# Attention stage scheduled in units of one pair of score maps, and its large loads issued by ScalarE

## What is computed

```
# sb (stick-breaking): 4 heads of 64
z = q k^T / 8
log_keep = where(k < q, log_sigmoid(-z), 0)
a = where(k < q, exp(log_sigmoid(z) + sum of log_keep over later keys), 0);   o = a v
# df (differential): 4 heads with two maps of 32 columns each
s = q_c k_c^T / sqrt(32) + bias;  p_c = softmax(s, chunk mask);   o = rmsnorm((p_0 - lam p_1) v) * g
# ds (top-k sparse): s = q k^T / 8 + bias, softmax over the keys the indexer chose
# fx (forgetting): s = q k^T / 8 + decay, causal softmax
x = x + concat(o_sb, o_df, o_ds, o_fx) w_out
```

## Time and profile before

| | us |
|---|---|
| median of 3 runs | 3913.75 (3907.92 to 3913.81) |
| the profiled execution's own time | 3915.1 |
| its span | 3913.3 |
| PE busy in the span | 3586.7 (92%) |
| DVE busy | 2494.6 (64%) |
| ACT busy | 1063.1 (27%) |
| attention, first layer | 662 to 1097 |
| attention, second layer | 2564 to 2998 |

### The profile page before, as it was taken

The page is one execution under the profiler, slowest core; times in us unless marked ns, Lnnn a source line. Parts: engine busy times, 40 slices in busy tenths (PEclk is TensorE's granted clock), DMA queues, the critical chain, the costliest instruction groups (busy, mean ns, idle before and its releaser), DMA issues. The chain is left out here.

```text
span 3913.3 us, 53493 instructions
## 1 busy us (share of the span) xinstructions
PE 3586.7 (92%) x19553; PEld 2727.3 (70%) x19553; DVE 2494.6 (64%) x4584; ACT 1063.1 (27%) x2223; POOL 34.4 (1%) x160
## 2 busy tenths in 40 slices
PE   4999998989878999999969999989998799999995
PEld 2554554656558999999935555555565699999994
DVE  3288996575654666655636899936655566655655
ACT  3111122565532111111111112145544311111112
POOL 0000000000000000000000000000000000000000
PEclk7999999899999999999989999988999899999997
DMA  4111214101001111111011221131100111111101
GB/s 164 69 41 64 69 41 160 62 7 48 20 11 60 49 48 36 45 48 48 12 63 55 69 70 43 59 121 59 48 12 23 44 46 35 48 48 48 48 27 45
DMA packets 216658, 206.69 MB, mean 53 GB/s; under 512 B 23846, under 2 KB 193158, under 8 KB 214430
## 3 DMA queue, kind: packets, MB, share of 16 engines
q1 hardware_dynamic: 216478, 204.36, 16.1%
HBM read 159.41 MB, written 44.91 MB: 52 GB/s over the span
## 5 line engine op out<-in xcount | busy, mean ns | idle before, releaser
L1614 PE MATMUL psum<-h_split,gate_up_split 128*128 128x352 f32 x6336 | 1021.5, 322 | 44.2 <-DVE gate_up_split L1728 44.2
L1614 PEld LDWEIGHTS psum<-h_split,gate_up_split 128*128 128x128 f32 x6336 | 1013.5, 189 | 48.3 <-issue 46.9
L882 PE MATMUL psum<-arena 128*128 128x512 f32 (+4 forms) x2304 | 756.1, 486 | 0.0
L1758 DVE TENSOR_TENSOR arena<-arena,psum 128x352 f32<-128x352 f32 x1056 | 513.6, 521 | 318.0 <-PE psum L1614 318.0
L882 PEld LDWEIGHTS psum<-arena 128*128 128x128 f32 (+1 forms) x2304 | 413.0, 181 | 329.2 <-issue 290.8
L1614 PE MATMUL psum<-hid_split,down_split 128*128 128x352 f32 x3168 | 522.9, 325 | 11.1 <-DVE down_split L1728 11.1
L1614 PEld LDWEIGHTS psum<-hid_split,down_split 128*128 128x128 f32 x3168 | 516.4, 190 | 11.6 <-issue 11.6
L1021 DVE MAX8 top<-arena 128x8 f32<-128x384 f32 (+6 forms) x394 | 346.7, 880 | 13.5
L1022 DVE MATCH_REPLACE8 arena<-top,arena 128x384 f32<-128x384 f32 (+6 forms) x394 | 339.0, 861 | 0.0
L1484 DVE CUSTOM_DVE_ANT_0 arena<-psum,arena 128x128 f32<-128x128 f32 (+8 forms) x288 | 194.7, 705 | 194.4 <-PE psum L1250 88.2
L1250 PE MATMUL psum<-arena 64*128 64x512 f32 (+9 forms) x1040 | 226.7, 543 | 65.2 <-ACT arena L1395 34.0
(11 more groups left out here) (139 smaller groups left out, 2748.2 us busy)
## 6 DMA issues: line engine op xcount, KB each, us to landing
gate_up_raw<-in_w_gate SPq DMA_DIRECT2D x44, 512.0 KB, 3.7
gate_up_raw<-in_w_up SPq DMA_DIRECT2D x44, 512.0 KB, 4.7
down_raw<-in_w_down SPq DMA_DIRECT2D x44, 512.0 KB, 3.5
arena<-in_w_in SPq DMA_DIRECT2D x24, 768.0 KB, 6.7
arena<-k_turned SPq DMA_DIRECT2D x8, 1184.0 KB, 5.7
k_turned<-arena SPq DMA_DIRECT2D x72, 128.0 KB, 2.2
q_turned<-arena SPq DMA_DIRECT2D x64, 128.0 KB, 2.1
arena<-bias_strips SPq DMA_DIRECT2D x4, 2048.0 KB, 10.2
```

The costliest lines, as they stand in the source:

```text
L882: ins = nc.tensor.matmul(m.ps[0:n, o + n0:o + n1], m.hT[:, c, c0:c0 + n], w[:, c, n0:n1], start=(c == 0), stop=(c == KC - 1))
L1614: ins = nc.tensor.matmul(out, w[i], x[k], start=(first and n == 0), stop=(last and n == 2))
L1758: nc.vector.tensor_tensor(x, x, bank(m, down_bank[p])[:, 0:PIECE], ALU.add).then_inc(s.added, 1)
```

## The change

A unit of one pair of maps (in df: one head) becomes the step of every loop. There are 90: ds 0 to 17, df 18 to 53, fx 54 to 71, sb 72 to 89. Scores run two units ahead (`AHEAD`), the weights (exp, combine, scan and multiply) one; sb's sigmoids, which free the score banks, also run two ahead. For that `soft` becomes a ring of four, the scan works in place in it and `back` goes. The fillers are spread over units 21 to 52 and 60 to 81. The group loads and `w_out` are issued by ACT: df and two parts before its loop, fx at unit 24, a part and sb at unit 57, the last part at unit 84. SP keeps the q blocks. The sigmoid set is asked for at v = 70, the iteration in which unit 72's sigmoids begin.

```diff
-FILLED = dict(ds=(21, 36), df=(41, 62))
+FILLED = dict(ds=(21, 53), df=(60, 82))
+AHEAD = 2
...
+                    for part in range(2 if g == "df" else 1):
+                        heads = [part] if g == "df" else [0, 1]
+                        self.units.append(Unit(len(self.units), st, heads, x, part == 1 or g != "df"))
+                        x += 2
...
@@ sync @@
             for e in range(3):
                 load_q(e)
-            load_group("df", 1, l)(sp, s.group_in1)
-            for g in ("ds", "df"):
-                load_w_out(m, a, l, g)(sp, w_out_in[W_OUT_SLOT[g]])
-            for e in range(3, n_steps // 2):
-                if e == 14:
...
-                    load_group("fx", 0, l)(sp, s.group_in0)
-                if e == 23:
...
-                    load_group("sb", 1, l)(sp, s.group_in1)
-                if e == 24:
...
-                    load_w_out(m, a, l, "fx")(sp, s.w_out_in0)
+            for e in range(3, len(steps) // 2):
+                sp.wait_ge(s.scored, 2 * steps[2 * (e - 2)].unit0)
                 load_q(e)
...
@@ tensor @@
-            for j in range(-1, n_steps + FLUSH):
-                scores(plan.step(j + 1), 0)
-                turn_probs(plan.step(j), 0)
-                weighted_sum(plan.step(j - 1), 0)
-                scores(plan.step(j + 1), 1)
-                turn_probs(plan.step(j), 1)
-                weighted_sum(plan.step(j - 1), 1)
-                sum_squares(plan.ended_at(j - 3, "df"))
-                turn_recips(plan.ended_at(j - 1, "ds", "df", "fx"))
-                products(j)
+            for v in range(-AHEAD, plan.n_units + FLUSH):
+                scores(plan.unit(v + AHEAD))
+                turn_probs(plan.unit(v), 0)
+                weighted_sum(plan.unit(v - 1), 0)
+                turn_probs(plan.unit(v), 1)
+                weighted_sum(plan.unit(v - 1), 1)
+                sum_squares(plan.ended_at(v - 3, "df"))
+                turn_recips(plan.ended_at(v - 1, "ds", "df", "fx"))
+                products(v)
...
@@ scalar @@
-            def weights(st, part):
...
+            def weights(v, c):
+                u = plan.unit(v + 1)
+                if u and u.st.g != "sb":
+                    exp(u, c)
+                u = plan.unit(v + AHEAD)
+                if u and u.st.g == "sb":
+                    sticks(u, c)
...
+            load_group("df", 1, l)(nc.scalar, s.group_in1)
+            for g in ("ds", "df"):
+                load_w_out(m, a, l, g)(nc.scalar, w_out_in[W_OUT_SLOT[g]])
+            for v in range(-AHEAD, plan.n_units + FLUSH):
+                if v + AHEAD < plan.n_units and units[v + AHEAD].v == plan.first_stick // 2:
                     act.preload_act_table_set("sigmoid_and_others")
-                copy_probs(act, nc.scalar.copy, "act", plan.step(j), 0, s.kept_act)
-                weights(plan.step(j + 1), 0)
-                copy_probs(act, nc.scalar.copy, "act", plan.step(j), 1, s.kept_act)
-                weights(plan.step(j + 1), 1)
+                if v == 24:
+                    act.wait_ge(s.dve_scored, maps_before("df"))
+                    summed_before(act, "ds")
+                    load_group("fx", 0, l)(nc.scalar, s.group_in0)
+                if v == 57:
+                    wait_copied(act, plan.of["product", ("ds", 3 * KC - 1), 0][0])
+                    load_w_out(m, a, l, "fx")(nc.scalar, s.w_out_in0)
+                    act.wait_ge(s.dve_scored, maps_before("fx"))
+                    summed_before(act, "df")
+                    load_group("sb", 1, l)(nc.scalar, s.group_in1)
+                if v == 84:
+                    wait_copied(act, plan.of["product", ("df", 3 * KC - 1), 0][0])
+                    load_w_out(m, a, l, "sb")(nc.scalar, s.w_out_in1)
+                weights(v, 0)
+                copy_probs(act, nc.scalar.copy, "act", plan.unit(v), 0, s.kept_act)
+                weights(v, 1)
+                copy_probs(act, nc.scalar.copy, "act", plan.unit(v), 1, s.kept_act)
...
@@ vector @@
-                scores(plan.step(j + 1), 0)
-                combine(plan.step(j), 1)
-                copy_probs(dve, nc.vector.tensor_copy, "dve", plan.step(j), 0, s.kept_dve)
-                scores(plan.step(j + 1), 1)
-                combine(plan.step(j + 1), 0)
-                copy_probs(dve, nc.vector.tensor_copy, "dve", plan.step(j), 1, s.kept_dve)
+            for v in range(-AHEAD, plan.n_units + FLUSH):
+                scan_sticks(plan.unit(v + 1), 0)
+                score(plan.unit(v + AHEAD), 0)
+                copy_probs(dve, nc.vector.tensor_copy, "dve", plan.unit(v), 0, s.kept_dve)
+                scan_sticks(plan.unit(v + 1), 1)
+                score(plan.unit(v + AHEAD), 1)
+                for c in range(2):
+                    weigh_sticks(plan.unit(v + 1), c)
+                combine(plan.unit(v + 1))
+                copy_probs(dve, nc.vector.tensor_copy, "dve", plan.unit(v), 1, s.kept_dve)
```

More of the change, by code:

```diff
@@ L52 @@
 PROB_RING = 6
+COPIED_BY_ACT = ("df", "sb")
 KC = D_MODEL // P
@@ L1041, in __init__ @@
     def __init__(self):
-        self.steps, unit, x = [], 0, 0
+        self.steps, self.units, x = [], [], 0
         for g in ATTEND_ORDER:
@@ L1059, in __init__, with unit @@
                 self.of.setdefault((kind, of, a), []).append(t)
[L1060 to L1070, removed]
+        self.first_stick = 2 * next(u.v for u in self.units if u.st.g == "sb")
+    def unit(self, v):
+        return self.units[v] if 0 <= v < self.n_units else None
@@ L1072, in fills_at, with ended_at, turns_at @@
+    def ended_at(self, v, *groups):
+        u = self.unit(v)
+        return u.st if u and u.last and u.st.hp == 1 and u.st.g in groups else None
+    def fills_at(self, v):
         for g, (a, b) in FILLED.items():
-            if a <= j < b:
-                return g, range(3 * KC * (j - a) // (b - a), 3 * KC * (j - a + 1) // (b - a))
+            if a <= v < b:
+                return g, range(3 * KC * (v - a) // (b - a), 3 * KC * (v - a + 1) // (b - a))
         return None, ()
-    def turns_at(self, j):
-        s = self.step(j)
-        for a in range(2 if s else 0):
+    def turns_at(self, v):
+        u = self.unit(v)
+        for a in (u.heads if u else ()):
+            s = u.st
@@ L1497, in weigh_sticks, with combine @@
                 dve.wait_ge(s.scanned, i + 1)
                 p = prob(x)[0:n, 0:keys - 1]
-                nc.vector.tensor_tensor(p, p, left[:, 1:keys], ALU.mult).then_inc(s.weighed, 1)
-            def scores(st, part):
-                if st is None:
+                nc.vector.tensor_tensor(p, p, m.soft[0:n, i % 4, 1:keys], ALU.mult).then_inc(s.weighed, 1)
+            def combine(u):
+                if u is None or u.st.g != "df":
                     return
-                x, h = plan.heads(st)[part]
-                if st.g == "sb":
-                    weigh_sticks(st, x)
-                elif st.g == "df":
-                    score(st, x, h)
-                    score(st, x + 1, h)
-                else:
-                    score(st, x, h)
```

207 lines of the change are left out of this document (96 added, 111 removed).

## The result

The changed kernel is slower: 3932.1 us (median of 5, 3929.0 to 3933.1) beside 3913.8 of the kernel before (median of 5, 3907.9 to 3913.9). The ratio is 1.005, 95% interval 1.0035 to 1.0064. The profiled execution has a span of 3931.3 us, against 3913.3.

What follows compares the result with a forecast made beforehand. PE was taken to bound ds and fx, handovers sb, with PE idle 10.9 us in df. Per layer -16 - 8 + 2 + 6 + 1.5 + 3.5 = -11, two layers -22: 3892 us, 8-in-10 range 3868 to 3912.

Steps and rivals of the forecast that it cites:

- sb, fillers and table loads: sb and fx's end: scores two ahead and fillers moved out of fx, -16 per layer; four extra table loads, +3.5.
- df: df: one unit more slack removes PE's waits behind ACT's squares and the combine, -8 us per layer (0 to -10.9).
- fx load on ACT: df's second block, unit 24: ACT held 9.3 us by issuing the load, 3.3 covered, +6 per layer (0 to +9).
- sb load on ACT: Unit 57: sb load and w_out, five issues of 0.55, 2.8 us, half hidden, +1.5 per layer.
- start: Attention's start: loads delay ACT's first exp by 7.7; q wait's 4.2 and prepared units' 1.5 offset it, net +2 per layer.
- The slack is about one unit: df, unit 24: work prepared ahead covers 3.3 us of ACT's 9.3 us hold; a unit there takes 2.9.
- The queue costs decide: Rival, chance 0.12: ACT's load stalls and table loads, 24.9 per layer uncovered, and a slower clock outweigh the gains: 3930.
- waits that go: df: fillers' waits behind ACT's squares, 5.6 in 5, and PE's short waits behind the combine were to disappear.
- the rest of the 10.9: df, 790 to 900 us: PE idle time outside the named waits was taken as the weight loads' own waits.
- Only sb gains: Rival, chance 0.16: df stays bound by the PSUM reader, -3 per layer, 3908.
- The clock stays up in df's start: Rival, chance 0.12: deeper lookahead shortens df's 30 us at half clock by some 10, -21 per layer, 3872.
- The q wait stays: Rival, chance 0.1: q loads share DMA engines with large loads, block 3's 4.2 us isn't won, -7 per layer, 3900.

Runs made afterwards that it cites:

- experiment 1: The changed kernel with every large load, those of w_out among them, back on SP in its old place: 3892.2 us, ratio 0.994 to before.
- experiment 7: Both exps of unit 71 before the first sigmoid, so one table load: on the changed kernel 3924.6 us, on experiment 1's kernel 3892.8 us.
- experiment 6: The changed kernel with the second set of fillers ending at unit 80, not 82, so none in large sb units: 3926.1 us, ratio 1.003.
- experiment 2: The changed kernel with the fx load alone back on SP, at q block 14: 3901.5 us, ratio 0.996 to before.
- experiment 3: The changed kernel with ACT issuing the fx load's five transfers one at a time, at units 24, 27, 30, 33 and 36: 3904.9 us, ratio 0.998.
- experiment 9: Changed kernel with loads on SP, no filler in large sb units, one table load, and ds fillers only in units without a weighted sum: 3869.9 us.
- experiment 5: The changed kernel with ACT's first load held until the first three q blocks have landed: 3933.0 us, ratio 1.005.
- experiment 10: Experiment 9's kernel with df's data and two w_out parts issued by SP at q block 6: 3851.5 us; the same in the kernel before: 3898.3 us.

## Why the prediction was wrong

The sum was -11 us per layer; the groups give +7.2. By its own terms:

| term, us per layer | forecast | measured | from |
|---|---|---|---|
| sb, fillers and table loads | -12.5 | -13.4 | fx, sb, tail: before 200.1, experiment 1 186.7 |
| df | -8 | +1.2 | df: 145.0, 146.2 |
| fx load on ACT | +6 | +14.3 | df: experiment 1 146.2, after 160.5 |
| sb load on ACT | +1.5 | +6.1 | fx, sb, tail: 186.7, 192.8 |
| start | +2 | -1.0 | entry and ds: before 87.6, after 86.6 |

**Right: sb, in its sum.** The period of 896 keys (6.35 and 6.44 for 6.2 to 6.5), the sigmoid wait (2.1 for "under 8"), the scores of 1024 keys at 1.99, five table loads and a sum right to a microsecond. That the sum is so near is in part luck, for it hides errors of both signs. The table loads, taken at 3.5, cost 1.9 and 2.7 in the stage (experiment 7, loads on SP). And fillers in the large units, taken for a gain of 1, cost 4.2 (experiment 6), because the copy that frees their bank now stands behind both maps' sigmoids. I had followed the move of the copy for the next scores only, and not for the next user of banks 4 and 5.

Two terms turned the sign, and neither alone: the fx load came out 8.3 us worse than forecast and df 9.2, while the sum had been -11.

**Wrong: the fx load.** The step that failed is "The slack is about one unit", and with it "9.3 - 3.3 = +6". The hold was sized right, 8.7 us (forecast 9.3), and so was its place. The price was 14.3, more than the hold itself. Experiments 2 and 3 show that it hangs on this load, and on its coming in a burst. Of slack there was next to none: PE's idle time in it was 7.89 us. (The 3.3 had no row; the 2.9 us of a unit beside it would have given +6.4.) The step ended with PE's restart, while the trace shows filler matmuls at twice their time behind it and a mean clock of 0.70 over 752 to 790, where experiment 1 has 0.87. The windows over df split the 14.3 in halves: PE is idle 19.6 us of 160.5 for 12.5 of 146.2, and busy 140.9 for 133.7 with the same work, at a clock of 0.85 for 0.91. The range's upper end for this term, +9, left the clock out; I had named it only in the rival "The queue costs decide". This rival gave 3930 and the measured time is 3932; it was priced with nothing covered, a slower clock and no gain in df, and those are what came true at unit 24 and in df. Its other half, the start, did not: there the hold and q's gain did cancel. So its 3930 is the right number by a sum that is half right.

**Wrong: df's -8.** The step that failed is the list of "waits that go". The fillers' wait behind the squares went (5.6), but PE's short waits behind the combine, which were to go too, doubled (2.7 to 5.3 over df), and the reader of PSUM rose from 2.1 to 5.4. PE's idle time in df was 12.6 us before and is 12.5 in experiment 1. Nor was "the rest of the 10.9" the weight loads' own: from 790 to 900 the waits view of before names engines for 10.3 of it. The rival "Only sb gains" had the main reason, the reader of PSUM. I had set it aside because that wait was small in the trace of before, and had taken even fillers as cover. But half of df's units have no weighted sum, and an even spread leaves those the shortest. Experiment 9 puts the fillers there and has 134.5 in the first layer and 137.3 in the second, -10.5 and -7.6 against before: the term of -8 could be had, by another placing. The clock's part in it was in no term. "The clock stays up in df's start" came true once the loads were off ACT (0.87 for 0.60), and brought nothing by itself, for the clock fell later in df.

**Wrong by less: the sb load**, +6.1 for +1.5, of which 4.4 to 5.5 stay when the fx load is on SP (experiment 2). 2.8 us of issue were assumed, 5.3 measured, for its last two transfers waited too (2.65 and 1.05), with PE's idle time and some low clock behind them (0.84 from 924 to 935).

**Start.** The forecast's q wait of block 3 went, as said, and ACT's first exp came at 677.6 for "near 674". Not foreseen: q block 0 itself landed 8.6 us later behind megabytes that another engine had issued 0.1 us after it. "The q wait stays" was the rival for this and had the wrong block. The Trainium skill (DMA: Bandwidth & Descriptors, Issuing engines are not separate DMA queues) says that transfers of different engines run on the same 16 DMA engines, and that another issuer saves only issue time, "which is usually small relative to the DMA itself". The trace agrees with the first half (11 us for 2.4, and 2.4 again once ACT's loads waited, experiment 5). On the second, the time in the issues was 8.7 us here, and moved to the engine that could least spare it.

Experiment 1 lands on the forecast's 3892, but by other terms than its own: without the loads' cost and without df's gain.

The kernel of experiment 10, 3851.5 us, beats both: 62 us under before, 81 under the change. Its layer takes 399.5 us for 434.5, of which fx, sb and the tail give 17.3 (the deeper order, with the fillers and the table load put right), df 10.4 and ds 7.4. Two layers would give 70; 6 to 8 of that are lost outside of attention, which the prediction had taken not to move ("a microsecond saved in attention is one saved in the span").

## What to carry to other kernels

A burst of transfers of megabytes held its issuing engine until earlier ones had moved (8.7 us here); give such a burst to an engine that nobody waits for, or issue its parts apart. Price a stall of PE with the matmuls behind it, which may run at half clock: here that doubled the price. Place filler work in the steps where the bounding engine has least of its own, and check each bank's next user, not only the scores', when a copy changes its place. Issue large loads when small urgent ones are through: here the small ones waited behind them from either engine.

## What was not expected of the hardware

- A 128 KB transfer issued 0.1 us ahead of megabytes from another engine took 11 us for 2.4.
- One edit without any new work, the fillers' place, gave 9 us of PE's busy time in the first layer, at a clock of 0.97 for 0.91, and only 2.6 through idle time (6 and 3 in the second).
- The same 8 us stall of ACT cost df 14.3 us in the order that had reached the higher clock, and 2.7 in the one that ran at the lower level there anyway.
- Five table loads took 1.28 us each, with the next activation 0.02 us behind (1003.15 + 1.28 = 1004.43, next at 1004.45). The Trainium skill (ScalarE: Activation LUTs, What ACT_TABLE_LOAD costs) puts a switch at about 2.66 us with the drain; no row here shows the other half.
- Gains of separate edits did not add: -6 and -7.5 us alone, none to be measured once the loads were off ACT's queue: 2.6 us per layer in attention, and as much lost outside of it.
